# A hybrid Fourier / attention / gated-linear-attention step: where two pairs of modulation tiles and the sums of quarters stand

## The reference

```python
mod = (silu(cond) @ w_mod + b_mod)          # 6 * 1024 columns
h = rms_norm(x, g1) * (1 + scale1) + shift1
z = h @ w_in                                # ... its last 3 * 1024 columns are zgate
y_a = fourier(zf) @ w_o_fourier
y_b = attention(...) @ w_o_mla
y_c = gated_linear_attention(...) @ w_o_gla
g = sigmoid(zgate)                          # three gates of width 1024
merged = g[0] * y_a + g[1] * y_b + g[2] * y_c
x = x + gate1 * (merged @ w_out)
h2 = rms_norm(x, g2) * (1 + scale2) + shift2
x = x + gate2 * (relu(h2 @ w_ff1) ** 2 @ w_ff2)
```

## Time and profile before

| | |
|---|---|
| median of three runs | 2078.44 us (2077.35 to 2079.84) |
| profiled execution | 2079.84 us |
| its span in the trace | 2078.0 us |
| TensorE busy | 1986.8 us, 96% |
| VectorE busy | 1211.9 us, 58% |
| ScalarE busy | 947.8 us, 46% |
| GpSimd busy | 265.1 us, 13% |
| mean granted TensorE clock | 0.986 of full speed |
| DMA | 195.92 MB, mean 94 GB/s |

### The profile page before, as it was taken

One profiled execution on the slowest core, in us unless ns is written; L12 is line 12 of the kernel. 1 busy time (PEld: TensorE's weight loads), 2 busy tenths in 40 slices (PEclk: granted clock), 3 DMA queues, 4 the chain that ended last, 5 costly groups with the idle time before them and its releaser, 6 DMA issues.

```text
span 2078.0 us, 34104 instructions
## 1 busy us (share of the span) xinstructions
PE 1986.8 (96%) x13976; PEld 1815.7 (87%) x13976; DVE 1211.9 (58%) x2099; ACT 947.8 (46%) x1758; POOL 265.1 (13%) x213
## 2 busy tenths in 40 slices
PE   5999999999998999999999999999999899999997
PEld 3985688899887999999989766888999799999997
DVE  4245688755567373736553456976564764646464
ACT  5525544434365162525454355453442743535262
POOL 0000000332002130403100000003220112121210
PEclk9999999999999999999999999999999999999999
DMA  9210011344422324242432100113543121313121
GB/s 364 73 51 11 1 36 42 127 153 152 168 79 104 143 83 150 73 146 90 156 108 73 39 3 1 47 62 116 170 151 132 41 82 62 102 62 102 62 93 60
DMA packets 53035, 195.92 MB, mean 94 GB/s; under 512 B 6032, under 2 KB 8144, under 8 KB 52112
## 3 DMA queue, kind: packets, MB, share of 16 engines
q1 hardware_dynamic: 49408, 174.61, 25.3%
q0 software_dynamic: 3472, 19.14, 2.6%
HBM read 187.79 MB, written 5.93 MB: 93 GB/s over the span
## 4 chain that ended last, share of the span: by engine, by line
PE 83%; DVE 9%; ACT 4%; issue 2%; DMA 1%; SPq 1%; ACTq 0%; DVEq 0%
PE ps L730 38%; PE ps L882 23%; PE ps L902 3%; PE ps L797 2%; PE ps L1048 2%; PE ps L911 2%; PE ps L748 2%; PE ps L1024 2%; PE ps L835 2%; DVE w_lo_parts L1670 2%; PE ps L1078 2%; PE ps L1053 1%; DMA w_raw<-in_stream 1%; ACT scratch L1495 1%; DVE scratch L2078 1%
## 5 line engine op out<-in xcount | busy, mean ns | idle before, releaser
L1670 DVE TENSOR_TENSOR w_lo_parts<-w_raw,w_hi_parts 128x512 fp32r<-128x512 f32 x548 | 405.8, 760 | 264.2 <-ACT w_hi_parts L1262 152.8
L1262 ACT CAST w_hi_parts<-w_raw 128x512 fp32r<-128x512 f32 x296 | 172.1, 619 | 453.3 <-PE ps L730 412.3
L730 PE MATMUL ps<-hid_hi_parts,w_hi_parts 128*128 128x320 f32 x1216 | 280.4, 312 | 4.6 <-DVE merged L2138 4.0
L730 PE MATMUL ps<-hid_lo_parts,w_hi_parts 128*128 128x320 f32 x1216 | 277.0, 309 | 0.0
L730 PE MATMUL ps<-hid_hi_parts,w_lo_parts 128*128 128x320 f32 x1216 | 276.9, 309 | 0.0
L1868 DVE SCALAR_TENSOR_TENSOR x<-ps,modulation,x 128x128 f32<-128x128 f32 (+2 forms) x216 | 81.7, 434 | 317.8 <-PE ps L730 317.8
L730 PEld LDWEIGHTS ps<-hid_hi_parts,w_hi_parts 128*128 128x128 f32 x1216 | 201.8, 188 | 27.6 <-issue 21.8
L1266 ACT CAST w_hi_parts<-w_raw 128x512 fp32r<-128x512 f32 x252 | 151.0, 621 | 128.3 <-PE ps L730 59.7
L730 PEld LDWEIGHTS ps<-hid_lo_parts,w_hi_parts 128*128 128x128 f32 x1216 | 203.3, 188 | 0.0
L730 PEld LDWEIGHTS ps<-hid_hi_parts,w_lo_parts 128*128 128x128 f32 x1216 | 203.2, 188 | 0.0
L882 PE MATMUL ps<-h_hi_parts,w_hi_parts 128*128 128x320 f32 x560 | 174.0, 311 | 2.1 <-DVE w_lo_parts L1670 2.0
(11 more groups left out here) (333 smaller groups left out, 4147.0 us busy)
## 6 DMA issues: line engine op xcount, KB each, us to landing
w_raw<-in_stream SPq DMA_DIRECT2D x312, 512.0 KB, 3.6
scratch<-in_first SPq DMA_DIRECT2D x10, 512.0 KB, 14.3
small_weights<-in_small POOLq DMA_DIRECT2D x2, 2048.0 KB, 11.5
h_scratch<-in_first SPq DMA_DIRECT2D x6, 512.0 KB, 17.0
x<-in_xT POOLq DMA_DIRECT2D x2, 1280.0 KB, 11.6
x<-in_xT POOLq DMA_DIRECT2D x8, 320.0 KB, 3.2
x_kept<-x POOLq DMA_DIRECT2D x8, 320.0 KB, 2.5
x<-x_kept POOLq DMA_DIRECT2D x8, 320.0 KB, 3.3
```

Source lines behind the costliest of these rows:

```text
L730: ins = mm(out[:, h, :], weight(w, s, k), a[:, k, h * HALF:(h + 1) * HALF], start=(first and n == 0), stop=(last and n == 2))
L1262: copy(place(wh, r), raw_half(s, n)).then_inc(w_hi, 1)
L1670: return tt(dst, full, hi.bitcast(F32), ALU.subtract)
```

## The change

It has three parts.

1. `mods_after`: in the mixing part a pair stands behind every m's q=0, as before, and one behind m0q1, in place of those behind m3q2 and m7q2. In the output projection the pairs start behind OUT0 in place of OUT1. The number of pairs per layer stays the same. The condition for the first feed-forward tiles is only written in another way.
2. VectorE's order: the four sums of quarters come after `gate_scratch_free` is raised, ahead of m=0, in place of before and between the steps of the concatenation; two differences come ahead of each of the two splits of m=0; the low parts of the differences come behind the multiplies of m=0 (0 and 1 behind b=0, then 2, then 3).
3. Only the last of the four sums is linked.

```diff
--- before.py
+++ after.py
@@ -81,10 +81,10 @@
     l, i = divmod(s, PER)
     if MIX0 <= i < OUT0:
         m, q = divmod(i - MIX0, 3)
-        return int(q == 0 or q == 2 and m in (3, 7))
-    if OUT0 < i <= OUT0 + (4 if l == 0 else 2):
+        return int(q == 0 or (m, q) == (0, 1))
+    if OUT0 <= i < OUT0 + (5 if l == 0 else 3):
         return 1
-    if l == 0 and i - FF0 in (1, 2):
+    if l == 0 and FF0 + 1 <= i < FF0 + 3:
         return 1
     if l == 0 and FF0 + KT < i < FF0 + 48:
         return int((i - FF0) % 16 in (9, 10, 12, 13))
@@ -1732,7 +1732,7 @@
             def quarter_in_full(n):
 
                 ins = tt(diff(True, n), quarter(hh, *QUARTER[n]).bitcast(F32), quarter(hl, *QUARTER[n]).bitcast(F32), ALU.add)
-                if n >= 1:
+                if n == 3:
                     e.link(ins)
 
             def make_diff(mix, n):
@@ -2084,17 +2084,11 @@
                         ins.then_inc(score_sb, 1)
                     gate_splits(G_LEVELS + GATE_LEVEL * (lv - 1), min(G_LEVELS + GATE_LEVEL * lv, G_LAST))
 
-                quarter_in_full(0)
-                quarter_in_full(1)
-                make_diff(True, 0)
                 dve.wait_ge(og_mm, e.at(og_mm, 1))
                 for k in range(6):
                     dve.wait_ge(cat_hi, e.at(cat_hi, k + 1))
                     low(ul[:, k, :], M[:, k, :], uh[:, k, :]).then_inc(cat_ready, 1)
                 gate_splits(G_LAST, 2 * KT * KT)
-                quarter_in_full(2)
-                make_diff(True, 1)
-                make_diff(True, 2)
                 dve.wait_ge(og_rstd, e.at(og_rstd, 1))
                 for t in range(2):
                     e.link(stt(M[:, 6 + t, :], OT[:, t, :], vl(e.layer, V_GG + t), OR[:, t, :], ALU.mult, ALU.mult))
@@ -2106,16 +2100,15 @@
                 dve.wait_ge(cat_ready, e.at(cat_ready, KT))
                 dve.sem_inc(gate_scratch_free, 1)
 
+                for n in range(4):
+                    quarter_in_full(n)
                 for m in range(KT):
                     i, o = MIX0 + 3 * m, O_MIX + 5 * m
                     for q in range(2 if m == 0 else 0):
+                        make_diff(True, 2 * q)
+                        make_diff(True, 2 * q + 1)
                         split_next(i + q)
                         modulation(i + q)
-                        if q == 0:
-                            quarter_in_full(3)
-                            make_diff(True, 3)
-                            low_diff(True, 0)
-                            low_diff(True, 1)
                     if m > 0:
                         for n in range(SEVEN):
                             pair_step(e.layer * PER + i, o, n, (G[:, 1, :], G[:, 2, :]))
@@ -2144,7 +2137,7 @@
                         if b == 2:
                             tt(out, out, halves(tmp), ALU.add).then_inc(gate_scratch_free, 1)
                         if m == 0:
-                            for n in ((2,), (3,), ())[b]:
+                            for n in ((0, 1), (2,), (3,))[b]:
                                 low_diff(True, n)
                         if m == KT - 1:
                             for k in ((0, 1, 2), (3,), ())[b]:
```

## The result

The changed kernel takes 2113.18 us (median of four runs, 2108.79 to 2115.62) where the kernel before took 2078.84 beside it (2077.35 to 2079.84, four runs): ratio 1.0164, 95% interval 1.0145 to 1.0181, so it is slower. The profiled execution took 2111.2 us, its span is 2109.4, against 2079.84 and 2078.0 before.

A forecast was written before the change was run, and what follows sets the result against it. TensorE, busy for 96% of the span, was taken to bound the kernel. The terms sum to 14.6 us per layer, twice 29.2, on a median of 2078.44 us, giving 2107.6 us, with a range of 2090 to 2114.

The forecast's parts named there:

- Links and quarters out of idle time: VectorE ahead of m=0: dropping links and taking quarter work out of idle time gains 0 (at most 0.03 us).
- The split's end T: Block m=0: VectorE's split of the wo tile, which frees its raw slot, ends at 373.3 instead of 366.9.
- The first pair: Block m=0: TensorE waits for the moved pair's tiles ahead of the wo product; fifth product +9.0 us, bounds 6.5 and 12.4.
- m=1: Mixing, block m=1: TensorE waits 0.9 us for the third of three tiles, bounds 0 and 2.3.
- m=3, m=4, m=7: Mixing: pair (3,2) leaves, -1.0 us; m=4's wait for its pair goes, -0.2; m=7 waits 0.6 for a low part.
- OUT: Output projection: TensorE waits one whole transfer between pairs 17 and 18, +3.6 us, plus 1.7 us for the clock.
- Nothing gives it back: Later stages follow TensorE, so none of the forecast loss is regained there.
- A: Rival: the m=0 wait comes, the OUT wait does not; 9.3 us per layer, 2097.0 us; chance 0.10.
- B: Rival: only OUT waits, the m=0 pair is in time; 7.6 us per layer, 2093.6 us; chance 0.07.
- C: Rival: transfers hidden in both places, only VectorE's lateness counts; 2.3 us per layer, 2083.0 us; chance 0.07.
- D: Rival: faster, the 2.01 and 1.03 us waits and m=4's 0.2 go; 3.2 us per layer, 2072.0 us; chance 0.06.
- E: Rival: VectorE's quarter work costs nothing, pairs only change places; within 0.2%, 2078.4 us; chance 0.02.

The follow-up runs named there:

- experiment 5: The changed kernel with the links behind the sums of quarters put back: 2110.9 us, ratio 1.0158 to the kernel before.
- experiment 8: The changed kernel, but GpSimd fetches x's first tile in block m=1 only when the pair has landed: 2111.81 us, ratio 1.0154.
- Experiment 2: First kernel: the changed one with the pairs around the output projection put back, 2100.18 us; second: the kernel before with only that part, 2096.21 us.
- order alone: VectorE's new order and the single link, with the pairs where the kernel before had them: 2089.84 us, ratio 1.0042.
- experiment 1: VectorE's new order without the new pair places, 2089.84 us, and the kernel before with only the new pair places, 2096.1 us.
- experiment 7: The kernel before with low parts of differences 0 and 1 moved behind b=0's multiply, 2079.0 us; with only difference 1's moved there, 2078.31 us.
- the changed kernel again: The changed kernel, unedited, run once more beside the kernel before: 2113.25 us, ratio 1.0156.
- experiment 3: The changed kernel with unread filler matmuls ahead of both waits, 12 calls in m=0 and 5 at the output projection: 2108.34 us, ratio 1.0148.
- experiment 4: The changed kernel, but VectorE splits the wo tile ahead of the four sums of quarters: 2113.38 us, ratio 1.0172.

## Why the prediction was right, point by point

**What bounds the kernel.** Right: instructions and bytes are the same, and the whole change is in TensorE's waits and the clock behind them.

**Links and quarters out of idle time: 0.** Right for the links (experiment 5), though miscounted: the diff takes away two of three in each layer (those behind the second and third sum), not three of four. The quarters taken away earlier moved nothing: the concatenation's last low part, begins 9.70 us behind line 1181's start before (361.59-351.89) and after (362.95-353.25).

**The split's end T.** Predicted 373.3, measured 374.63 in a layer that began 1.36 us later: 373.3. This is the one number that makes the wait long, and it came from counting steps of one form.

**The first pair.** Right in place, cause and size: +9.0 predicted, +8.9 measured. Part of that closeness is luck, since within it two errors cancel. The transfer took 4.88 us from T (374.63 to 379.51) where the row of m=4 had given 5.3; the clock cost 0.9 on the pair and 1.2 on the next 48 matmuls, 2.1 where I had 1.7. The page "DMA: Bandwidth & Descriptors" of the Trainium skill (section "Anatomy of one DMA"), by whose fit for the software path I had estimated 4.4 us for two tiles, is about as far off on the other side as my row. The VectorE chain that I followed step by step was met too: TensorE waited 0.18 us (0.72 in layer 1) for its fifth weight where I had 0.5. The first low part took 2.08 us beside GpSimd, the next 1.48: +0.6, as taken.

**m=1.** The right wait, mis-sized. The term was 0.9 and the wait measured 1.63 and 3.17 us; with the clock 1.9 and 4.7. The step at fault is "5.5 us (one step past the second)" for the third of three tiles: from the slot's release at 398.19 the three issues take 0.9 us one behind the other, the transfer 5.16, and 0.14 pass until the matmul, 6.2 in all. That gives 1.6, which is layer 0. Layer 1's transfer took 6.75 us, and its 4.7 us lie outside the bounds of 0 to 2.3 us; why some transfers take that long is open. The x tile fetched beside it is not shown to be the cause, and a transfer of instructions goes with it (experiment 8). Of the 4.7 us, 1.6 are the low clock, which did not fall behind such a wait everywhere (last section). This term is nearly all of the difference between my 29.2 us and the 33.7 of the two stages.

**m=3, m=4, m=7.** -1.2 predicted, -1.4 to -1.5 measured; the low part's wait 0.6 predicted, 0.70 measured.

**OUT.** Right: 3.6 predicted, 3.71 and 3.68 measured, released by TensorE's pair just ahead; clock 1.7 predicted, 1.6 measured. Experiment 2 shows that this term stands by itself.

**"Nothing gives it back".** Right within what a run shows: 2.3 us of 33.7.

**The range.** It held narrowly. My terms' upper bounds made 2122 and I cut the top to 2114; one of the four executions, 2115.62, lies above it. The forecast was 29.2 us over before and the medians are 34.3 apart.

**The rivals.** A and B each lacked a wait that came; the first kernel of experiment 2, which is A made real, was 16 us (by the ratio) to 18 us (by the medians) over the kernel before, where A had 18.6. C was in part right as a mechanism and wrong in price: I had +2.9 us for VectorE's lateness alone up to the fifth product, and order alone cost 5.0 to 5.8, since a wait of 1.54 us came back behind it and the clock fell there too. D needed T at 365 and it was 373.3 on before's scale. E fell with experiment 1.

## What to carry to other kernels

In a ring that is filled strictly in order, write out for each moved tile which old tile must be used up first, and who uses it up: a tile moved forward by two places can wait for an engine that it had nothing to do with. Idle time of an engine is worth using where it lies: work taken out of it and put ahead of a step that releases a transfer costs its own length and then uncovers the transfer's, so count the two one behind the other. Removing one wait is worth only the distance to the next one on the same engine: in experiment 7 the next one stood a few products further on, so look there before booking it.

## What the runs showed of the hardware

- In the profile after, the granted clock was 0.50 behind the wait of 8.7 us and 0.57 behind that of 3.7. With fillers, and 2.26 us of the longer wait left, it still fell to 0.78 and then 0.50; with 0.95 us left it stayed at 1.00. The length of the wait alone does not tell: at m=1 the clock fell to 0.50 behind 3.17 us (the profile after, 1446 to 1448) and stayed at 1.00 behind 3.06 us in two other profiles (the changed kernel again, 1450.6 to 1458; experiment 3, 404.8 to 412). In the kernel before, the 2.01 us of the earlier trace rows left it at 1.00 (windows 376 to 380). I had not expected 2.26 us to be enough behind fillers that kept TensorE busy for 6.62 us.
- Three tiles of 512 KB released together: the second landed 4.9 us behind the release (in m=0), the third 6.1 us (in m=1), and in layer 1 7.6 us behind it (1437.08 to 1444.69), with a packet of instructions on another DMA queue in that stretch; four of five such long cases have one and none of the thirteen short ones.
- VectorE's three differences of 1.49 us each took 6.46 us in experiment 4, and two of GpSimd's sums beside them 2.13 and 2.39 us, against 1.26 and 1.28 with VectorE idle in the profile after.
